# Seven of eight merge-gate tiles per branch inside the branch's own stage, the eighth in the merge

## The reference, cut to what matters

```python
pc = split_proj(u_c @ w_in[l]); px = split_proj(u_x @ w_in[l])
# branches: gated DeltaNet (scan over chunks), Hyena (long convolutions),
# GQA and differential attention; then, per token:
def merge_branches(ys, merge_logits, w_br, w_out):
    y = jnp.stack(ys, axis=-2)
    proj = jnp.einsum('blnw,nwd->blnd', y, w_br)
    g = jax.nn.sigmoid(merge_logits.reshape(*merge_logits.shape[:-1], N_BRANCH, D_MODEL))
    return jnp.sum(g * proj, axis=-2) @ w_out
```

## Time and profile before

| | us |
|---|---|
| median of 3 runs | 3329.32 (3328.86 to 3331.95) |
| the profiled execution, its own time | 3333.73 |
| span of the profiled execution | 3331.9 |
| PE busy | 2976.4 (89%) |
| PEld busy | 2375.9 (71%) |
| DVE busy | 1658.3 (50%) |
| ACT busy | 968.4 (29%) |
| POOL busy | 637.4 (19%) |

### The profile page before, as it was taken

The page is one execution under the profiler, slowest core; times in us unless marked ns, Lnnn a source line. Parts: engine busy times, 40 slices in busy tenths (PEclk is TensorE's granted clock), DMA queues, the critical chain, the costliest instruction groups (busy, mean ns, idle before and its releaser), DMA issues.

```text
span 3331.9 us, 39966 instructions
## 1 busy us (share of the span) xinstructions
PE 2976.4 (89%) x16126; PEld 2375.9 (71%) x16126; DVE 1658.3 (50%) x2853; ACT 968.4 (29%) x1402; POOL 637.4 (19%) x262
## 2 busy tenths in 40 slices
PE   7898999798898989998979989889979989999977
PEld 1387989776787877786766438788867767777765
DVE  5546676525333432334546644667734445343545
ACT  0333222221222233214422234322222233322433
POOL 0021000020122211221113312100022232132126
PEclk9898999899999999999988999899989999999988
DMA  6410000112322112210124541000023331131124
GB/s 230 152 45 20 26 23 31 51 65 90 101 91 89 64 40 81 82 57 26 53 87 128 186 166 51 17 20 20 23 88 121 119 109 42 61 126 39 57 86 148
DMA packets 104598, 259.21 MB, mean 78 GB/s; under 512 B 11906, under 2 KB 35076, under 8 KB 104032
## 3 DMA queue, kind: packets, MB, share of 16 engines
q1 hardware_dynamic: 98474, 236.32, 21.2%
q10 hardware_dynamic: 5942, 20.33, 1.7%
HBM read 219.89 MB, written 36.70 MB: 77 GB/s over the span
## 4 chain that ended last, share of the span: by engine, by line
PE 77%; DVE 13%; ACT 4%; issue 2%; DMA 2%; POOL 1%; SPq 1%; ACTq 0%; DVEq 0%; POOLq 0%
PE ps L752 16%; PE ps L753 15%; PE ps L754 15%; PE ps L760 11%; PE ps L899 4%; PE ps L1206 3%; PE ps L857 2%; PE ps L1140 2%; PE ps L812 2%; PE ps L1233 1%; PE ps L1230 1%; DMA t_raw<-in_w_ada 1%; PE ps L1216 1%; DVE t_gcv L1764 1%; ACT t_whi L1320 1%
## 5 line engine op out<-in xcount | busy, mean ns | idle before, releaser
L713 POOL TENSOR_TENSOR t_wlo<-t_raw,t_whi 128x1024 fp32r<-128x1024 f32 x248 | 612.9, 2474 | 2663.4 <-ACT t_whi L1320 2663.4
L752 PE MATMUL ps<-t_u_hi,t_whi 128*128 128x512 f32 (+1 forms) x2368 | 898.4, 379 | 81.3 <-ACT t_a_gst L1378 32.2
L753 PE MATMUL ps<-t_u_lo,t_whi 128*128 128x512 f32 (+1 forms) x2368 | 842.4, 356 | 0.0
L754 PE MATMUL ps<-t_u_hi,t_wlo 128*128 128x512 f32 (+1 forms) x2368 | 839.7, 355 | 0.0
L752 PEld LDWEIGHTS ps<-t_u_hi,t_whi 128*128 128x128 f32 x2368 | 456.1, 193 | 169.3 <-issue 84.7
L1320 ACT ACTIVATE t_whi<-t_raw 128x1024 fp32r<-128x1024 f32 x248 | 261.9, 1058 | 1026.0 <-PE ps L754 846.9
L754 PEld LDWEIGHTS ps<-t_u_hi,t_wlo 128*128 128x128 f32 x2368 | 452.8, 191 | 65.8
L753 PEld LDWEIGHTS ps<-t_u_lo,t_whi 128*128 128x128 f32 x2368 | 456.1, 193 | 59.1 <-issue 7.4
L760 PE MATMUL ps<-t_grp 128*128 128x128 f32 x3008 | 383.8, 281 | 34.8 <-DVE t_grp L2032 11.7
L760 PEld LDWEIGHTS ps<-t_grp 128*128 128x128 f32 x3008 | 369.7, 196 | 54.7 <-issue 31.1
L1378 ACT ACTIVATE t_grp<-ps 128x512 f32<-128x512 f32 x236 | 138.1, 597 | 401.5 <-PE ps L760 334.6
(11 more groups left out here) (245 smaller groups left out, 3702.8 us busy)
## 6 DMA issues: line engine op xcount, KB each, us to landing
t_raw<-in_w_in SPq DMA_DIRECT2D x184, 512.0 KB, 3.5
t_raw<-in_w_ada SPq DMA_DIRECT2D x48, 512.0 KB, 4.3
t_raw<-in_w_br SPq DMA_DIRECT2D x32, 512.0 KB, 4.4
t_raw<-in_w_out SPq DMA_DIRECT2D x32, 512.0 KB, 3.9
t_sg<-gate_logits SPq DMA_DIRECT2D x32, 384.0 KB, 4.2
hs<-t_hstage ACTq DMA_DIRECT2D x20, 512.0 KB, 3.6
t_hring<-hs SPq DMA_DIRECT2D x20, 512.0 KB, 5.6
t_raw<-in_fwd SPq DMA_DIRECT2D x128, 64.0 KB, 2.4
```

The source lines that it names most:

```text
L713: pool.tensor_tensor(wlo[:, c % CONV, :], raw[:, s % RAW, :], whi[:, c % CONV, :].bitcast(f32), ALU.subtract).then_inc(sems["w_ready"], 1)
L752: pe.matmul(o, lh, rh, start=first, stop=False)
L753: pe.matmul(o, lh, rl, start=False, stop=False)
L754: return pe.matmul(o, ll, rh, start=False, stop=last)
```

## The change

Per branch seven tiles (`WOVEN`) stay in the stage, the eighth is computed in the merge. In the merge it is a fifth projection into a PSUM slot, after the four of the branch's gate; ACT takes the sigmoid straight from PSUM into `t_sg`, without store and load. Of the seven:

- DeltaNet: one at the end of `gdn_project`, whole, behind the last projection and ahead of the turn of its result; four woven into the scan in steps; two (`LAST_TILES`) behind the scan's last phase, ahead of `out_norm`'s turns.
- Hyena: six whole tiles in the convolutions (in layer 0 the one between the two inverses goes, in layer 1 one of the two there), the seventh behind the last projections.
- GQA: all seven in attention, by `between`: whole units, spread over all phases.
- Differential attention: five in attention by `between`, two behind its last item.

ACT takes the root of `out_norm` behind the first of the two last tiles, and waits for all stores to land behind the second. The sum of the log decays in `gdn_project` moves from j = 4 to j = 6. The weight stream follows.

ACT around the first merge of layer 0, before: four silus, then the sigmoids of loaded logits between the splits of weights.

The diff, cut to its core:

```diff
@@ convolution
     yield "inv", 0, 0
-    yield "gate", 0, 0
     if l:
         yield "gate", 0, 0
@@
+        WOVEN, LAST_TILES = KT - 1, 2
+        def steps_by(l, p, phases, n):
+            return min(p, phases - 6) * n * gate_units(l) // (phases - 6)
+        def units_by(l, p, phases, n):
+            return p * n * len(segs(l == 0)) // phases
@@ gate_loads (SP)
-                    sp.wait_ge(gl_st[i], 16 * (stored[0] // 2))
+                    sp.wait_ge(gl_st[i], 16 * ((stored[0] + 1 - i) // 2))
                 for d in range(KT):
-                    sp.dma_start(sg[:, d, 0:w], logits[l, n, d, :, 0:w]).then_inc(sg_ld[d // 4], 16)
+                    if d < WOVEN:
+                        sp.dma_start(sg[:, d, 0:w], logits[l, n, d, :, 0:w]).then_inc(sg_ld[d // 4], 16)
                     pieces(1)
+                pieces(1)
@@ (PE)
+            def between(l, main, steps, phases, tiles_in):
+                n = 0
+                for p, _ in enumerate(main):
+                    while n < units_by(l, p + 1, phases, tiles_in):
+                        for _ in range(KT):
+                            next(steps)
                         n += 1
                 for _ in steps:
                     n += 1
@@ gdn_project (PE)
-                    if j == 4:
+                    if j == 6:
...
+                for _ in range(gate_units(l)):
+                    next(gates)
                 after(11)
@@ merge (PE)
                 for j in range(BT):
                     project(full, "mg_sil")
+                freed["mg_sg"] = freed.get("mg_sg", 0) + WOVEN
+                project(full, "mg_sg")
                 ln.take("mg_y", BT)
@@ hyena (PE)
                 for j in range(4):
                     project(full, "cv_done")
+                for _ in gates:
+                    last = "the seventh tile"
                 ln.take("hy_z1", 4)
@@ attend (PE)
-                weave(l, main(), (7,), 3 * len(its))
+                between(l, main(), gate_steps(l, (7,)), 3 * len(its), WOVEN - (LAST_TILES if diff else 0))
@@ layer loop (PE)
-                gdn_project(l)
+                steps = gate_steps(l, (6, 7))
+                gdn_project(l, steps)
                 fence(ln, "pe")
-                weave(l, gdn_scan(l), (6, 7), SCAN_PHASES)
+                weave(l, gdn_scan(l), steps, SCAN_PHASES, WOVEN - LAST_TILES - 1)
@@ out_norm (ACT)
+                for _ in segs(l == 0):
+                    next(evacs)
                 ln.take("on_ss")
+                ln.done(run(ss[:, 1, 0:n], ss[:, 0, 0:n], ACT.Sqrt, scale=1.0 / HD, bias=eps), "on_sd")
+                for _ in evacs:
+                    last = "the tiles behind the last round"
                 for i in range(2):
-                    act.wait_ge(gl_st[i], 16 * (units[0] // 2))
-                ln.done(run(ss[:, 1, 0:n], ss[:, 0, 0:n], ACT.Sqrt, scale=1.0 / HD, bias=eps), "on_sd")
+                    act.wait_ge(gl_st[i], 16 * ((units[0] + 1 - i) // 2))
@@ merge (ACT)
-                for d in range(KT):
+                for d in range(WOVEN):
...
-                    if d % 2 and d > 1:
-                        pieces_used(1)
-                pieces_used(1)
+                pieces_used()
+                ln.done(run(sg[:, WOVEN, 0:w], next_slot()[:, 0:w], ACT.Sigmoid), "mg_sg")
+                pieces_used(4)
```

More of the change, by code:

```diff
@@ L228, in stream_of @@
         if b == "gdn":
-            s += [("w", O_GDN + P * j) for j in range(12)] + gates
+            s += [("w", O_GDN + P * j) for j in range(12)] + gates[:7]
         if b == "hyena":
@@ L649, in _ @@
                 pieces(12)
-                for j in range(KT):
+                for j in range(WOVEN):
                     pieces(1)
@@ L670, in _ @@
                 pieces(4)
+                if late:
+                    gate_stores(l, 1, tile)
+                    tile += 1
+                pieces(1)
+                gate_stores(l, 1, tile)
                 fenced(f0 + 6)
@@ L796, in gate_steps, with weave @@
                             yield
[L798 to L800 removed]
+            def weave(l, main, steps, phases, tiles_in):
+                n = 0
                 for p, _ in enumerate(main):
[L802 removed]
+                    while n < steps_by(l, p + 1, phases, tiles_in):
                         next(steps)
+                        n += 1
+                for _ in steps:
+                    n += 1
+            def between(l, main, steps, phases, tiles_in):
+                n = 0
+                for p, _ in enumerate(main):
+                    while n < units_by(l, p + 1, phases, tiles_in):
+                        for _ in range(KT):
+                            next(steps)
                         n += 1
@@ L901, in half, with gdn_project @@
                 ln.done(last, name)
-            def gdn_project(l):
+            def gdn_project(l, gates):
                 full = l == 0
@@ L1149, in hyena @@
                                     lend("hy_inv", *((4, 5) if st else (2, 3, 4, 5)))
-                for _ in gates:
-                    raise ValueError("gate tiles left over")
                 for j in range(4):
                     project(full, "cv_done")
+                for _ in gates:
+                    last = "the seventh tile"
                 ln.take("hy_z1", 4)
@@ L1358, in gate_evacs, with weave @@
                         yield
-            def weave(l, main, evacs, phases):
+            def weave(l, main, evacs, phases, tiles_in):
                 n = 0
                 for p in range(phases):
-                    while KT * (n + 1) <= steps_by(l, p, phases):
+                    while KT * (n + 1) <= steps_by(l, p, phases, tiles_in):
                         next(evacs)
@@ L1367, in weave, with between @@
                     next(main)
-                for _ in evacs:
-                    n += 1
+                for _ in range(n, tiles_in * len(segs(l == 0))):
+                    next(evacs)
+                for _ in main:
+                    raise ValueError("phases left over")
+            def between(l, main, evacs, phases, tiles_in):
+                n = 0
+                for p in range(phases):
+                    while n < units_by(l, p, phases, tiles_in):
+                        next(evacs)
+                        n += 1
+                    next(main)
+                for _ in range(n, tiles_in * len(segs(l == 0))):
+                    next(evacs)
                 for _ in main:
@@ L1696, in main @@
                         yield
-                weave(l, main(), gate_evacs(l, (7,), a_gst), 3 * len(its))
+                evacs = gate_evacs(l, (7,), a_gst)
+                between(l, main(), evacs, 3 * len(its), WOVEN - (LAST_TILES if diff else 0))
                 ln.due["at_pv"] = pv0 + len(its)
+                return evacs
             def project_out(l):
```

42 lines of the change are left out of this document (22 added, 20 removed).

## The result

The changed kernel takes 3252.36 us (median of 4 runs, 3247.82 to 3260.62); its ratio to the kernel before is 0.9763 (95% interval 0.9737 to 0.9789), so it is faster by some 79 us. The forecast was 3214 us, with a range of 3175 to 3266. The profiled execution of the changed kernel took 3260.6 us, with a span of 3258.8 and a mean granted clock of 0.959 (0.949 before).

A forecast was written before the change was run, and what follows sets the result against it. PE, busy 89% of the time, was taken as the bound, its work unchanged. Gains of 201 us less costs of 87 gave 114, called 115, taken from the 3329.3 us median: 3214 us, range 3175 to 3266.

The forecast's parts named there:

- A tile in the merge is the same 24 matmuls a segment: Premise that moving a tile from a stage into the merge takes nothing away from PE's work.
- 1, merges: Merges: the eighth tile fills PE's eight waits for t_b_lo, 45 us plus slow clock behind them; gain 66 us.
- 7, the end of hyena: End of hyena: the seventh tile covers two fence waits for DVE, about 10 us, 15 with the clock.
- 2 and 3: In gdn_project: later log decays remove their wait, 12.6 us; a tile at its end covers t_gsl waits, 16 us.
- (a): Scans: four tiles fewer woven in, 56 us, of which half turns to waiting; cost 28 us (14 to 45).
- term 4: Ends of scan and differential attention: two tiles cover waits, 58 us less 18 for ACT's hold; gain 40 (30 to 50).
- (b): Convolutions: the tile behind the first inverse is gone, so PE waits for t_y; cost 6 us.
- 5, 6: Attention: bank 7 waits go, gain 32 us; 180 fewer switches between single steps and phases, gain 20 (0 to 32).
- (c): Attention: items that no unit follows wait for their own softmax; cost 45 us (25 to 60).
- the slower rival: Attention: waits beside whole units drop PE's clock; 3400 us if half its work is slow; chance 5%.
- (d): Differential attentions: more slow-clock stretches from the short new waits; cost 8 us.
- The chains swallow what is moved out: Rival: ACT and DVE bound scans and attention, less filling uncovers waits; 3277 us; chance 17% together with a late merge.

The follow-up runs named there:

- e1_even: Changed kernel with one PSUM slot left out behind the merge's fifth projection, so each merge uses an even number: 3221.06 us, ratio 0.9651 to the kernel before.
- e2_before_odd: Kernel before the change with one slot left out in each merge and no tile moved: 3368.75 us, ratio 1.0099 to the kernel before.
- e7_merges: Only the eighth merge tile and hyena's order, even slots; scan and attention tiles in single steps, none at their ends, decays at j = 4: 3271.65 us, ratio 0.9817.
- e6_j4: e1_even with the sum of the log decays back behind projection j = 4: 3240.69 us, ratio 0.9716 to the kernel before.
- e5_noends: e1_even with no tile at the ends of gdn_project, scan and differential attention: 3251.87 us, ratio 0.9747 to the kernel before.
- e4_conv: e1_even with a tile back between layer 0's two inverses, from the pair ahead of the context's inverse: 3198.83 us, ratio 0.9587 to the kernel before.
- e3_weave: e1_even with gate tiles handed out in single steps, not whole units, in both attentions: 3219.34 us, ratio 0.9651 to the kernel before.
- e8_half: e4_conv with half units (4 steps) in place of whole ones in both attentions: 3168.96 us, ratio 0.9502 to the kernel before.

## Why the prediction was right in sign and in mechanism, and 38 us off

- **"A tile in the merge is the same 24 matmuls a segment".** True of the work, and here the forecast failed: it costed the fifth projection by its matmuls alone and priced the rest at nothing. The projection also takes a slot, and the slots are handed out by a count that the next stage goes on with. e1_even puts this at 37 us, e2_before_odd at 33. With these 37 the forecast of 3214 would be 3251, where 3252 was measured. That this comes out so closely is luck, as the misses of the other terms, listed below, cancel. No rival named the slot.
- **1, merges, 66, with 7, the end of hyena, 15.** Confirmed as one: 61 (51 to 71) in e7_merges against 65, which is 66 + 15 less 6 for `t_y` and 10 for a tile less in each of four stages. No run takes the merges alone. Of 7, the waits of 5.9 and 4.4 us for DVE at hyena's last fence went, and 1.5 and 1.7 for ACT stand there now.
- **2 and 3, log decays and the end of gdn_project, 12.6 + 16.** From the first projection to the scan's first matmul the kernel before takes 157.4 and 145.4 us, the changed one 151.0 and 137.7 with a tile of 8.4 and 5.6 more in it. That is 28.1 us gained against 28.6. e6_j4 puts 11.4 of them down to the decays. In e5_noends the stretch takes 151.1 and 138.3 without the tile: at this place the tile costs nothing.
- **3 and 4, the ends, against (a).** The terms stood at 16 + 40 - 28, and 9 more for the items uncovered; e5_noends gives 32 (17 to 46) for the part of them it undoes, where the same terms, with three tiles put back, give 26. The waits fell as forecast. Of ACT's hold for the stores I took 4.5 us at each end; between the turns 1.4 to 2.1 are seen, 7.1 in all, and 1.3 for DVE (`t_gtok`, `t_atok`). So term 4 took off 18 us where 8.4 are seen.
- **(a), scans.** Four tiles less, 56 us. The stretch to the last scan matmul was 317.26 and 298.11 before, 298.37 and 283.58 after: 33.4 came back and 22.6 did not, against 28. Of the 22.6, 12.6 are more idle time of PE (length less busy time), and some 5 are the clock of layer 0, which fell from 0.99 to 0.97 (an estimate: 17 us at half speed in place of 7). The forecast had no term for this: in all nine runs with four tiles in the scan of layer 0 its clock is 0.96 to 0.98, in the three with five or seven it is 1.00. The slope is not even: by e5_noends the last tiles of seven cost little in layer 0 (3.5 us each of 8.4, the clock's help in it) and nearly all in layer 1 (4.8 of 5.6). The 0.54 from which the half was taken is not sound. It stands on "some 35 us less of PE's gate work", but by the forecast's own tile length eight tiles differ by 22.4 us, and of the 304 matmuls that layer 1 has less only 192 are gate steps'. With 22.4 the slope would have been 0.85. That a half came near the measured 0.60 is luck.
- **(b), convolutions.** 6 was forecast and 8.1 measured at `t_y`, but taking it away gave 21 us (e4_conv): the wait for `t_h_gst` (10.4, against 8.9 before) and the clock hung on the same order. The term was the wrong size because it read one wait and not the clock behind it.
- **5, 6 and (c), attention.** Each was there: bank 7 fell from 32.2 to 2.7, the bare items have the period of 4.9, and the windows came within 3.4 us of the forecast's. The forecast gave the sum +7 and e3_weave measured 0. For the switches, the time from start to start, without idle time, of all gate and projection steps in GQA of layer 0 with its merge, over all rows of PE, is 111.1 us before, in 66 groups, and 102.1 after, in 15, for the same 192 steps: 0.18 a switch, as in the earlier trace rows. e8_half, with 105.0 in 29 groups, gives 0.2. The Trainium skill's statement in "TensorE: Matmul & The Clock Gate", "Step-by-step: what each phase is for", that the next weights load while a matmul runs, does not make such switches free here.
- **The clock in attention.** It stayed at 0.93 to 1.00; the slower rival falls, as e3_weave wins nothing by a finer weave. (d) took 8 us for more slow stretches: over the four attentions the time at the lower clock rose from 32 to 41 us, which costs half of the difference, some 4 (an estimate).
- **The chains swallow what is moved out.** Its time, 3277, lies 25 us from the measured one, nearer than the forecast with its 38. That is chance: its mechanism fell, as the scan gave back 60%, and what made the time longer than forecast was the slot.

## What to carry to other kernels

When an operation is added to a stage, count what it takes besides its time: a slot, a buffer, a parity, a place in a ring that the next stages go on with, and ask which buffer the first operation of the next stages will now be given. Filling work pays in the size of the hole that it fills: an item with a chain of 4.9 us and 3.5 us of own matmuls wants two steps, not eight and then none (the differential attention of layer 1, 92.3 us against 108.4). And where busy time grows with the same matmuls, look inside the rows: a wait within a group of instructions shows as busy.

## What the runs showed of the hardware that was not expected

An addition on DVE takes 1.22 us in the kernel before, where it starts alone. In the changed kernel the same one takes 3.42, at both convolutions of layer 0; DVE's timeline:

```profile
802.57 3.42 DVE L1808 TENSOR_TENSOR t_oT<-t_oT 128x1024 f32<-128x1024 f32 x1
806.03 1.22 DVE L1808 TENSOR_TENSOR t_oT<-t_hcv,t_hring 128x1024 f32<-128x1024 f32 x1
```

and POOL's:

```profile
802.53 2.38 POOL L725 TENSOR_TENSOR t_wlo<-t_raw,t_whi 128x1024 fp32r<-128x1024 f32 x1 [29.66 <-ACT t_whi L1348]
```

POOL's instruction began 0.04 us earlier, and DVE's ended 1.08 us behind its end: it looks as if DVE did next to nothing while POOL's ran. That made the wait for `t_y` 3.9 us and not the 1.8 of the earlier trace rows.

It is not new with the change, only its place is. In layer 1 of the kernel before, an addition on DVE begins first and takes its usual 1.22 us, POOL's, begun 0.52 us behind it, takes 2.95 in place of some 2.4, and DVE's next one, begun while POOL's runs, takes 3.29:

```profile
2550.19 1.22 DVE L1756 TENSOR_TENSOR t_oT<-t_oT 128x1024 f32<-128x1024 f32 x1
2551.45 3.29 DVE L1756 TENSOR_TENSOR t_oT<-t_hcv,t_hring 128x1024 f32<-128x1024 f32 x1
```

```profile
2550.71 2.95 POOL L713 TENSOR_TENSOR t_wlo<-t_raw,t_whi 128x1024 fp32r<-128x1024 f32 x1 [3.44 <-ACT t_whi L1320]
```

This one too ends 1.08 us behind POOL's end, and so do others of this shape that begin up to 1.6 us into POOL's. An addition with one input in PSUM isn't held: in e4_conv the second of two (`t_hcv<-ps,t_h_odd`) begins at 788.86, 0.02 us behind POOL's, and takes 1.21.

The Trainium skill says so of two SBUF inputs on DVE against a GpSimd instruction ("SBUF — State Buffer", "SBUF: two separate sides"): whichever starts first has the shared pair of ports for its whole instruction, and the other waits. The trace agrees, in both orders; no run here takes POOL's instruction away from that place alone.
